# Attention with the keys on the partitions, and a state scan in four stretches side by side

## The reference

```python
# (A) grouped-query attention: 8 query heads on 2 key/value heads, head width 128
s = einsum('bgrqd,bgkd->bgrqk', q, k) * 128 ** -0.5
p = softmax(s, axis=-1)
y_a = einsum('bgrqk,bgkd->bgrqd', p, v) * silu(gate_a)

# (B) a bidirectional diagonal state-space layer: 64 groups, 64 complex states each
a_bar = exp(a * dt)
bu = einsum('blgp,gnp->blgn', u, b_bar)
# state[t] = a_bar * state[t - 1] + bu[t], forwards and backwards
y = y + einsum('blgn,gpn->blgp', states, c).real
```

## Time and profile before

| | |
|---|---|
| median of 3 runs | 2812.23 us (2809.74 to 2815.75) |
| the profiled execution | 2818.78 us, of which 2816.7 us is its span |
| PE busy over the span | 2561.4 us, 91% |
| DVE, ACT, POOL busy | 1419.5, 924.0 and 1134.4 us (50%, 33%, 40%) |
| stage `heads` | 548.6 to 905.5 us of the span |
| stage `s5_outputs` after it | 905.5 to about 1048 us |

### The profile page before, as it was taken

How to read it: one execution, slowest core, us unless ns; L and a number is a source line. 1 busy time by engine, 2 the same in 40 slices (tenths; PEclk the granted TensorE clock), 3 DMA queues, 4 the chain that set the end, 5 groups by cost and what they waited for, 6 DMA issues and landing times. The chain is left out here.

```text
span 2816.7 us, 41316 instructions
## 1 busy us (share of the span) xinstructions
PE 2561.4 (91%) x15638; PEld 2209.2 (78%) x15638; DVE 1419.5 (50%) x2285; ACT 924.0 (33%) x1916; POOL 1134.4 (40%) x1244
## 2 busy tenths in 40 slices
PE   6999997699998777899799999899899689999798
PEld 5988887589997666677588888777777579999687
DVE  6564444687887945322654453455555422222314
ACT  4232222633333233233322223356566400000331
POOL 3444441177776125412054554433333345553320
PEclk9999999999999888999899999999999799999899
DMA  7323333301111355444333333443423454442553
GB/s 162 114 61 106 106 106 82 64 24 47 32 39 31 61 108 169 144 166 147 116 100 129 117 145 126 133 164 107 167 96 130 174 169 145 147 145 90 172 172 149
DMA packets 268744, 328.33 MB, mean 117 GB/s; under 512 B 45684, under 2 KB 217358, under 8 KB 267414
## 3 DMA queue, kind: packets, MB, share of 16 engines
q1 hardware_dynamic: 230390, 239.10, 28.8%
q10 hardware_dynamic: 38176, 86.78, 8.3%
HBM read 212.75 MB, written 103.55 MB: 112 GB/s over the span
## 5 line engine op out<-in xcount | busy, mean ns | idle before, releaser
L1044 POOL TENSOR_TENSOR w_hi<-w_raw,ones 128x512 fp32r<-128x512 f32 (+1 forms) x232 | 277.2, 1195 | 771.3 <-PE r L1055 263.9
L1046 POOL TENSOR_TENSOR w_lo<-w_raw,w_hi 128x512 fp32r<-128x512 f32 (+1 forms) x232 | 342.0, 1474 | 18.2
L1055 PE MATMUL r<-h_lo,w_hi 128*128 128x264 f32 (+1 forms) x864 | 286.7, 332 | 0.0
L1055 PE MATMUL r<-h_hi,w_lo 128*128 128x264 f32 (+1 forms) x864 | 278.6, 322 | 0.0
L1055 PE MATMUL r<-h_hi,w_hi 128*128 128x264 f32 (+1 forms) x864 | 277.7, 321 | 0.0
L1055 PE MATMUL r<-xc_lo,w_hi 128*128 128x264 f32 (+1 forms) x768 | 248.8, 324 | 30.4 <-POOL w_lo L1046 30.4
L1055 PE MATMUL r<-xc_hi,w_lo 128*128 128x264 f32 (+1 forms) x768 | 249.4, 325 | 0.0
L1055 PE MATMUL r<-xc_hi,w_hi 128*128 128x264 f32 (+1 forms) x768 | 248.8, 324 | 0.0
L440 POOL TENSOR_TENSOR w_lo<-w_raw,w_hi 128x512 fp32r<-128x512 f32 x64 | 87.1, 1388 | 232.3 <-ACT w_hi L516 232.1
L1055 PEld LDWEIGHTS r<-xc_lo,w_hi 128*128 128x128 f32 x768 | 146.4, 191 | 43.1 <-issue 31.0
L1055 PEld LDWEIGHTS r<-h_lo,w_hi 128*128 128x128 f32 x864 | 163.0, 189 | 16.3 <-issue 2.4
(11 more groups left out here) (345 smaller groups left out, 6393.8 us busy)
## 6 DMA issues: line engine op xcount, KB each, us to landing
w_raw<-in_w_in_even SPq DMA_DIRECT2D x72, 256.0 KB, 3.0
w_raw<-in_w_in_odd SPq DMA_DIRECT2D x64, 256.0 KB, 3.5
w_raw<-in_w_ogate SPq DMA_DIRECT2D x64, 256.0 KB, 7.1
v_d<-vs ACTq DMA_DIRECT2D x8, 1152.0 KB, 4.2
us<-u_d SPq DMA_DIRECT2D x128, 65.0 KB, 3.1
xc_d<-xc ACTq DMA_DIRECT2D x8, 1040.0 KB, 6.5
qk_d<-qk ACTq DMA_DIRECT2D x16, 520.0 KB, 2.7
sz_d<-sz SPq DMA_DIRECT2D x8, 1040.0 KB, 5.2
```

Of the source, the lines that this page charges most:

```text
L1044: self.nc.gpsimd.tensor_tensor(hi, raw, one, ALU.mult).then_inc(self.hi_done, 1)
L1046: self.nc.gpsimd.tensor_tensor(lo, raw, hi.bitcast(F32), ALU.subtract).then_inc(self.split, 1)
L1055: ins = self.nc.tensor.matmul(bank[:, 0:n], w[:, u % self.buffers, k, :], z[:, off:off + n], start=(first and k == 0 and w is self.hi and ...
```

## The change

It rewrites `heads`, the scan, and the few lines of `front` and `s5_outputs` that feed them.

**Attention.** Work goes in 16 units (`NU`), two for each head: one of 580 queries (5 tiles of 116) and one of 460 (4 tiles of 115), called `long` and `short` here after their PSUM buffers. The keys are cut into nine tiles of 116 (`KEYS`, the last has 112), and a unit runs over them in nine slots. Counted in slots, for unit n:

- PE makes the scores of a key tile with the keys stationary and the queries moving, in `HALVES`: two halves of 290 columns, or one of 460. So the scores come out with keys on the partitions.
- ACT copies them to SBUF (`keep`). DVE reads the same PSUM region after that and keeps a running maximum over the key tiles in `top` (`higher`, slots 1 to 8). Each unit has two regions of its own kind in turn.
- In the next unit's time PE turns `top` (`turn_top`, slot 0), DVE reduces it to one maximum for each query (`find`, slot 1), and PE spreads those over the partitions again (`spread`, slot 2).
- From slot 3 to slot 8, and slot 0 of the unit after that, DVE subtracts the spread maximum from the nine kept tiles (`lower`), one or two for a slot by `LOWERED`, and ACT takes the exponential of each in place (`power`).
- Two units later PE multiplies with the values (`mix`): now the probabilities are stationary and the values move, 129 columns with a column of ones at the end. The output has queries on the partitions, and its last column is the sum.
- ACT takes the rows out (`take_rows`), DVE inverts the sum (`invert`), ACT scales (`scale_rows`), PE turns the rows back (`turn_rows`), and DVE multiplies them into the gate buffer (`out`), which SP stores.

SP now loads queries and gates by units. The stores of the result move from ACT's queue to SP's.

**Scan.** `Z` gets 132 slots behind its first, in four stretches of 33 (`SUPER`, `LONG`). A first pass scans all four together, 32 times; a second adds the ends (2 times), with a step for 33 slots called `far`; a third adds to each slot what the stretches before it brought, three stretches together, 32 times. Each time is one product with a step of four entries and two additions. It is written out without a loop. The table's scratch is the buffer `pw_in`, which `s5_outputs` now uses in the same way.

**Front.** DVE computes `far` with six complex products of six instructions each, and four more to store it. `vt` has 129 columns for each key head, and is cut by `KEYS`.

The core of the diff:

```diff
+KEYS = [(i * 116, min(116, L - i * 116)) for i in range(NT)]
+PARTS = [(0, 580, 5, 116), (580, 460, 4, 115)]
+START = (222, 0)
+HALVES = ([(0, 290), (290, 290)], [(0, 460)])
...
-            vt = se.sb("v", [P, NT, KV * HD])
+            vt = se.sb("v", [P, NT, KV, HD + 1])
...
-            t["Z"] = se.sb("Z", [P, CH + 1, 2, G])
+            t["Z"] = se.sb("Z", [P, 1 + SUPER * LONG, 2, G])
...
-    with do.loop(CH // 2, 8) as i:
-        for b in range(2):
...
-            do.free(tt(tmp[:, 0], now, t["step_re"][:, :, :], ALU.mult))
-            do(tt(tmp[:, 1], now, t["step_im"][:, :, :], ALU.mult))
-            do(tt(tmp[:, 0], tmp[:, 0], tmp[:, 1, ::-1, :], ALU.add))
-            gp.sem_inc(turns, 1)
-            do(tt(nxt, nxt, tmp[:, 0], ALU.add))
...
+    for j in range(1, LONG):
+        own, other = product(z[:, :, j - 1, :], "step")
+        now = halves(z[:, :, j, :])
+        add(now, now, own)
+        add(now, now, other)
+    for s in range(1, SUPER - 1):
+        own, other = product(z[:, s - 1:s, LONG - 1, :], "far")
...
+    left = z[:, 0:SUPER - 1, LONG - 1, :]
+    for j in range(LONG - 1):
+        own, other = product(left, "step")
+        add(carry[:, :, :, :], own, other)
+        left = carry[:, :, :, :].rearrange("p s o g -> p s (o g)")
+        now = halves(z[:, 1:SUPER, j, :])
+        add(now, now, carry[:, :, :, :])
...
+                one, power = (pw[:, T, 0, :], pw[:, T, 1, :]), (X(0), X(1))
+                times(power, one, one)
+                for n in range((LONG - 1).bit_length() - 2):
+                    times(power, power, power)
+                times(power, power, one)
...
+    LOWERED = {0: ((2, 8),), 3: ((1, 0),), 4: ((1, 1), (1, 2)), 5: ((1, 3),), 6: ((1, 4), (1, 5)), 7: ((1, 6),),
+               8: ((1, 7),)}
...
+                def scores(n, j):
...
+                    else:
+                        pe.wait_ge(kept, NT * n + j - 1)
+                        pe.wait_ge(raised, (NT - 1) * n + j - 2)
...
+                def mix(n, j):
...
+                    for x in range(j * tiles, (j + 1) * tiles):
...
+                for n in range(LAST + 1):
+                    for j in range(NT):
+                        if n < NU:
+                            scores(n, j)
+                        if j == 2 and 1 <= n <= NU:
+                            spread(n - 1)
+                        if 2 <= n < LAST:
+                            mix(n - 2, j)
+                        for w in turned_at.get(n * NT + j, ()):
+                            turn_rows(w, n)
+                        if j == 0 and 1 <= n <= NU:
+                            turn_top(n - 1)
...
+                for n in range(LAST + 1):
+                    for j in range(NT):
+                        for w in mixed_at.get(n * NT + j - 1, ()):
+                            take_rows(w)
+                        if n < NU:
+                            keep(n, j)
+                        for back, k in LOWERED.get(j, ()):
+                            if 0 <= n - back < NU:
+                                power(n - back, k)
+                        for w in mixed_at.get(n * NT + j - 1, ()):
+                            scale_rows(w)
...
+                def higher(n, j):
...
+                    dve.wait_ge(kept, NT * n + j + 1)
```

More of the change, by code:

```diff
@@ L1681, in _ @@
-                scores(0)
-                for n in range(NR + 1):
-                    if n + 1 < NR:
-                        scores(n + 1)
-                    if n < NR:
-                        turn(n)
-                    if n:
-                        mix(n - 1)
+                def scores(n, j):
+                    off, width, tiles, m = PARTS[n % 2]
+                    ko, kn = KEYS[j]
+                    g = n // 2 % KV
+                    if j == 0:
+                        pe.wait_ge(q_done, n + 1)
+                        if n >= 2:
+                            pe.wait_ge(found, n - 1)
+                        if n and turned_in[n - 1]:
+                            pe.wait_ge(yd, turned_in[n - 1])
+                    elif j == 1:
+                        if n >= 2:
+                            pe.wait_ge(low, NT * (n - 1))
+                    else:
+                        pe.wait_ge(kept, NT * n + j - 1)
+                        pe.wait_ge(raised, (NT - 1) * n + j - 2)
+                    out = region(n, j)
+                    for o, w in HALVES[n % 2]:
+                        for x, z in ((0, 1), (0, 0), (1, 0)):
+                            last = nc.tensor.matmul(out[0:kn, START[n % 2] + o:START[n % 2] + o + w],
+                                                    kr[z][:, g, ko:ko + kn], q[x][:, off + o:off + o + w],
+                                                    start=(z == 1), stop=(x == 1))
+                    last.then_inc(sc, 1)
@@ new lines, in turn_top @@
+                def turn_top(n):
+                    off, width, tiles, m = PARTS[n % 2]
+                    pe.wait_ge(kept, NT * n + 8)
+                    pe.wait_ge(raised, (NT - 1) * (n + 1))
+                    out = region(n, NT)
+                    for i in range(tiles):
+                        at = TOPS[n % 2][i]
+                        last = nc.tensor.transpose(out[0:m, at:at + KEYS[0][1]], top[0:KEYS[0][1], i * m:(i + 1) * m],
+                                                   c["ident"][0:KEYS[0][1], 0:KEYS[0][1]])
+                    last.then_inc(tt, 1)
@@ new lines, in spread @@
+                def spread(n):
+                    off, width, tiles, m = PARTS[n % 2]
+                    pe.wait_ge(found, n + 1)
+                    pe.wait_ge(kept, NT * (n + 1))
+                    out = region(n, NT + 1)
+                    for i in range(tiles):
+                        at = SPREAD_AT[n % 2] + i * m
+                        last = nc.tensor.transpose(out[0:KEYS[0][1], at:at + m],
+                                                   peak[0:m, i:i + 1].broadcast_to([m, KEYS[0][1]]),
+                                                   c["ident"][0:m, 0:m])
+                    last.then_inc(sp_done, 1)
@@ L1722, in _, with leading, keep @@
-                for b in range(2):
-                    act.wait_ge(stored[b], 16 * REP)
+                def leading(n):
+                    cols = columns(n, 1)
+                    act.wait_ge(ql[n % 2], 16 * (n // 2 + 1))
+                    if n >= 2:
+                        act.wait_ge(sc, NT * (n - 1))
+                    nc.scalar.activation(q[0][:, cols], qf[:, cols], ACT.Copy).then_inc(hid, 1)
+                def keep(n, j):
+                    kn, width = KEYS[j][1], PARTS[n % 2][1]
+                    if j == 0 and n >= NB:
+                        act.wait_ge(pv, DONE[n - NB + 1])
+                    act.wait_ge(sc, NT * n + j + 1)
+                    nc.scalar.activation(sb[0:kn, n % NB, j, 0:width],
+                                         region(n, j)[0:kn, START[n % 2]:START[n % 2] + width],
+                                         ACT.Copy).then_inc(kept, 1)
@@ new lines, in find @@
+                def find(n):
+                    off, width, tiles, m = PARTS[n % 2]
+                    dve.wait_ge(tt, n + 1)
+                    if n:
+                        dve.wait_ge(sp_done, n)
+                    out = region(n, NT)
+                    for at, i0, i1 in TOP_RUNS[n % 2]:
+                        ins = v.tensor_reduce(peak[0:m, i0:i1],
+                                              out[0:m, at:at + (i1 - i0) * KEYS[0][1]].rearrange(
+                                                  "p (i k) -> p i k", k=KEYS[0][1]), AX, ALU.max)
+                    ins.then_inc(found, 1)
@@ new lines, in out @@
+                def out(w, now):
+                    n, i = spot[w]
+                    off, width, tiles, m = PARTS[n % 2]
+                    if i == 0:
+                        dve.wait_ge(gl[n % 2], 16 * (n // 2 + 1))
+                    dve.wait_ge(tu, w + 1)
+                    y = gate[:, off + i * m:off + (i + 1) * m]
+                    v.tensor_tensor(y, y, region(now - 1, NT)[:, 0:m], ALU.mult).then_inc(yd, 1)
+                v.memset(vt[:, :, :, HD:HD + 1], 1.0).then_inc(ones_set, 1)
@@ new lines, in _ @@
+                rest(0)
+                for n in range(LAST + 1):
+                    for j in range(NT):
+                        if j == 1 and 1 <= n <= NU:
+                            find(n - 1)
+                        for w in mixed_at.get(n * NT + j - 1, ()):
+                            invert(w)
+                        for w in out_at.get(n * NT + j, ()):
+                            out(w, n)
+                        for back, k in LOWERED.get(j, ()):
+                            if 0 <= n - back < NU:
+                                lower(n - back, k)
+                        if n < NU and j:
+                            higher(n, j)
+                        if j == 5 and n + 1 < NU:
+                            rest(n + 1)
```

327 lines of the change are left out of this document (178 added, 149 removed).

## The result

| | before | after |
|---|---|---|
| median, us | 2811.06 (4 runs side by side) | 2792.34 (4 runs, 2791.14 to 2795.92) |
| ratio of the times | | 0.9929, 95% interval [0.9912, 0.9945] |
| the profiled execution, us | 2818.78 | 2791.14 |
| next stage begins at, us | 905.55 | 884.71 |

The change is faster by 18.7 us (0.7%). The time lies inside the predicted range of 2750 to 2803, but the forecast had 42.5 us: less than half of it came. The two profiled executions lie 27.6 us apart: the stage `heads` explains 20.8 us of it, and the other 7 us fall in later stages, 4.6 of them in one of the second layer (438.9 and 434.3 us), which the change leaves alone.

The account below looks back on a forecast made before the run. PE was taken as the bound, the scan about equally long. Attention ending at 861 and the scan at 859 put the stage's end at 863, 42.5 us off, so 2769.7 us; own range 2753 to 2799, with tails 2750 to 2803.

Parts of the forecast that it names:

- What bounds: `heads` and scan before the change: PE bound, scan just about equally long, ending 11.6 us ahead; both must shrink.
- PE's own work: PE in attention: scores 109 us, `mix` 145, transposes 22, sum 276 us against 339 before.
- rival 4: Attention at PE's bare 34.5 us a head and a cheaper POOL product: stage end near 838, 2745 us; chance 0.09.
- DVE and ACT per instruction: Attention passes: `lower` 0.757 and 0.632 us, `keep` 0.655 and 0.555; DVE 30.4, ACT 29.3 us a head.
- The unit of 18.3 us: Attention unit: 5.3 + 12.3 + 0.7 = 18.3 us, against 17.2 if PE alone set the pace.
- q's low part: DVE's pass of two SBUF inputs in attention waits for POOL, costing some 0.7 us more a unit.
- Slots 3 to 8: This part of an attention unit takes 12.3 us of either kind, PE's figure or DVE's with a little coupling.
- POOL: Scan: 304 us for 344.9 before, plus 6 us blocked by DVE, ending at 859.
- Front, ends, next stage: `front` 0, up to 20 us if stretched; first scores 554.0, units 0 and 1 until 579.4; `s5_outputs` 0.
- Rival 3: PE's clock falls to 1.2 GHz for a third of the stage: end about 950, 2857 us; chance 0.05.
- Rival 2: Every `lower` and `higher` on DVE shuts POOL out: scan ends at 1042, 2949 us; chance 0.03.
- Rival 1: DVE and ACT lock step in attention, 0.3 us more a slot: units 21 us, 2806 us; chance 0.11.

Follow-up runs that it names:

- last version: Changed kernel with the old scan's short instructions written out, at most one row turned a slot, q split in slots 0 and 1: 2754.87 us, ratio 0.98.

## Why the prediction was off, step by step

- **What bounds: half right.** PE did set the pace before. The scan was "just about equally long", but it was no bound, and the step that followed, "the stage shrinks only as far as both do", was true only as a limit: the scan as it was would have allowed an end at 873, 11 us ahead of what the changed kernel reaches.
- **PE's own work: right.** 276 us make 17.2 us a unit. `mix` had 0.111 us an instruction, 143 us in place of 145. The last version has 18.87 and 15.36 us in most of its units, 17.1 in the mean, with PE busy 39.76 of 40 us. I had called that pace an outer case, with a stage end at 846 in the range and at 838 in rival 4; it was 847.0.
- **DVE and ACT per instruction: right but for one.** `lower`, `higher`, `keep`, `power` within 2%.
- **The unit of 18.3 us: this is the step that failed.** It had 5.3 us for slots 0 to 2, 12.3 for 3 to 8 and 0.7 for the wait of q's low part. Slots 0 to 2 took 7.45 (mean over the seven `long` units with 8.16 and the six `short` ones with 6.63; so are the means below). 5.3 is the length of DVE's chain, and I did not hold PE's own work in these slots against it: by the same prediction it was 17.2 less 11.25 (the mean of its 12.3 and 10.2), 5.95. Measured with one row a slot it was 6.6. On top come 0.87 us, shown by the same run: two rows turned one after the other with a hand-over to DVE and back between them. The order of the program showed both; I had costed transposes as 0.103 us each.
- **Slots 3 to 8** would have been 11.3 us without POOL's part (1.0 under my 12.3), and were 12.4.
- **q's low part:** mis-sized. 0.7 us, from the median of another pass, in `front`; with the new scan it was 1.1 us a unit, the difference in slots 3 to 8 between the changed kernel and the one without a scan. I had sized POOL's instructions for the scan's end and not for what waits behind them. Together: 1.3 for PE's own work in slots 0 to 2, 0.9 for the two rows, 1.0 less in slots 3 to 8 and 0.4 for q make 1.6, the 1.6 us by which a unit was longer. That 12.3 was 1.0 too long is partly luck: it hid that much of the three other errors.
- **POOL: right** in price (854.1 for 859; products 2.40 and 1.84), and it bought nothing. I had counted the scan as a second thing that had to shrink; it had 11.6 us of slack, and written out in its old form it would have had more than the new one.
- **Front, ends, next stage: right.** The zeroing of `Z` starts 0.5 us off its time before, units 0 and 1 end 2.2 us late, the tail from unit 15 on took 44.5 us to the next stage. The price of 20 us for a stretched `front` was a slip: a third of 40 instructions at 1.3 us makes about 25. The term was taken at 0, and `heads` did begin at 548.5 us, as before.
- **Rival 3 (the clock)** came only in small, though a fall of PEclk in the middle was one of my signs of being wrong. The one fall in the middle of the changed kernel, 0.93 from 640 to 660 us, cost 1.6 us where this rival had priced 92; in the run with q split early the same thing cost about 9.
- **Rival 2** (DVE and POOL exclude each other) named the right pair of engines with the wrong instructions and looked at one direction: the 272 passes with an operand in PSUM did not slow POOL (its additions over 512 elements took 1262 to 1297 ns unless a low part of q ran beside them, up to 1873 then), and what cost time was the 16 passes from SBUF that waited for POOL. **Rival 1** (lock step, 2806) has a longer unit too, but the hand-overs between ACT and DVE that it named were not the cause: the last version has them all, and PE is full.

## What to carry to other kernels

Before lengthening the instructions of an engine that is off the critical path, list which instructions of its neighbour can wait for it, and add the wait to each: anything up to the whole of such an instruction, here 0.8 to 1.0 us in the mean beside instructions of 1.0 to 2.4. When a slot is costed as a chain of one engine, hold the bound engine's own work in the same slot against it, and count a serial hand-over wherever an instruction is issued twice in a slot through one buffer. An edit that does nothing may be covered by another loss: this one was worth 9 us once the two others were gone. And when a wait of PE is moved, compare the granted clock too: here the longer waits brought slower stretches behind them.

## What the runs showed of the hardware

Two kinds of DVE pass from SBUF to SBUF waited for the instruction that POOL had in progress and then ran, the low part of q and the normalising pass: a pass of four columns (155 ns at the least) took up to 2360 ns beside products of 2402 and 1844 in the mean, while the whole low part of q, 756 ns without a scan, never took more than 1065 beside instructions of 450. Nor did only passes with two SBUF inputs wait: the normalising pass has one, and went from 874 to 1609 ns. Passes with an operand in PSUM did not: `higher` over 580 columns took 757 ns with the long instructions and 758 without a scan. Nor did the inverse, which goes from SBUF to SBUF but for one column: no more than 167 ns in any run with the new attention, though 53 of the changed kernel's 72 lay wholly beside an instruction of POOL.
The Trainium skill ("SBUF — State Buffer", section "SBUF: two separate sides") calls the shared pair of ports "an exclusive lock, not a bandwidth split", held by whichever instruction starts first for its whole length. The traces agree, from the 2.06 us at 734.25 and the 2.35 us at 639.58, which both end about 0.6 us behind POOL's instruction. In the changed kernel every low part of q of 580 columns that was lengthened ended 0.616 to 0.620 us behind the end of POOL's instruction, every one of 460 columns 0.491 to 0.497, and in the run with four columns it was 0.018 to 0.024: the pass is held until POOL is done, and then needs 0.14 us less than its undisturbed 0.756, 0.631 and 0.155.
The loop, with its two semaphore increments a slot, also cost POOL something by itself: 520 instructions of the same kind ended at 872.9 in the loop and at 816.5 written out, 0.11 us an instruction, with the same attention beside them. Which part of it is the loop and which the increments, no run here shows.

TensorE's clock fell from 2.4 to 1.2 GHz in the middle of the stage only behind waits of PE: at 639 us of the changed kernel after 0.38 us of work in two (0.57 from 639 to 643), and at 743 us with q split early (0.50 from 744 to 746), as behind the waits at the other four falls of that run. Not every wait brought it: in the changed kernel slot 7 of unit 6 took 3.92 us, against 2.05 without a scan, at a granted clock of 1.00.
